# The end of attention in a two-layer block: output products in parts, weight splits placed last, a norm's chunks spread

## The reference, cut to what matters

```python
for l in range(DEPTH):                      # DEPTH = 2
    xn = _rms_norm(x, attn_norm[l])
    h = xn @ w_in[l]
    ...
    o_a = _dense_causal_attention(...)      # "mla", 4 heads of 64
    o_b = _dense_causal_attention(...)      # "fox"
    o_c = _moba_attention(...)              # "moba"
    o_d = _diff_causal_attention(...)       # "diff"
    o_d = _rms_norm(o_d, diff_sub_norm[l]) * (1.0 - lam_init)
    o_e = _memory_attention(...)            # "mem"
    mixed = jnp.concatenate([_merge(o_a), _merge(o_b), _merge(o_c), _merge(o_d), _merge(o_e)], axis=-1)
    x = x + mixed @ w_o[l]
    xn = _rms_norm(x, ffn_norm[l])
    gate = _causal_dwconv(xn @ ffn_w_gate[l], ffn_conv_w[l], ffn_conv_b[l])
    x = x + (jax.nn.silu(gate) * (xn @ ffn_w_up[l])) @ ffn_w_down[l]
return x
```

## Time and profile before

| | us |
|---|---|
| median of 3 runs | 2453.97 (2451.75 to 2454.61) |
| the profiled execution's own time | 2455.71 |
| its span | 2453.7 |
| PE busy | 2374.2 (97%) |
| DVE busy | 1803.3 (73%) |
| ACT busy | 1371.4 (56%) |
| POOL busy | 130.9 (5%) |

### The profile page before, as it was taken

How to read it: one execution, slowest core, us unless ns; L and a number is a source line. 1 busy time by engine, 2 the same in 40 slices (tenths; PEclk the granted TensorE clock), 3 DMA queues, 4 the chain that set the end, 5 groups by cost and what they waited for, 6 DMA issues and landing times.

```text
span 2453.7 us, 33655 instructions
## 1 busy us (share of the span) xinstructions
PE 2374.2 (97%) x14448; PEld 2117.4 (86%) x14448; DVE 1803.3 (73%) x1835; ACT 1371.4 (56%) x1347; POOL 130.9 (5%) x107
## 2 busy tenths in 40 slices
PE   5999999999999999999999999998998999998999
PEld 5999999788988888888888888876888999788999
DVE  5666566776688888888888888886575676665766
ACT  4345444464577777677777777765444344544433
POOL 2001000001100000000000000004110001201000
PEclk9999999999999999999999999999898999998999
DMA  5653546453499999999999999994233655332653
GB/s 191 190 188 122 188 149 223 129 195 123 157 365 354 355 345 348 351 358 347 353 348 357 347 356 350 355 342 138 82 108 103 206 173 178 112 104 72 194 182 104
DMA packets 309644, 566.92 MB, mean 231 GB/s; under 512 B 12338, under 2 KB 137553, under 8 KB 309360
## 3 DMA queue, kind: packets, MB, share of 16 engines
q1 hardware_dynamic: 305792, 560.39, 65.9%
q10 hardware_dynamic: 3696, 4.30, 0.5%
HBM read 563.60 MB, written 1.05 MB: 230 GB/s over the span
## 4 chain that ended last, share of the span: by engine, by line
PE 85%; DVE 7%; ACT 3%; DMA 3%; POOL 1%; issue 1%; ACTq 0%; DVEq 0%; SPq 0%; POOLq 0%
PE bank L996 22%; PE bank L787 15%; PE bank L1014 11%; PE bank L771 7%; PE bank L637 7%; PE bank L625 6%; PE bank L250 4%; PE bank L1317 3%; DVE wL L202 3%; PE bank L647 2%; PE bank L1266 2%; PE bank L613 2%; DMA raw<-in_od_moe_gu 2%; ACT wH L231 2%; DVE arena L202 1%
## 5 line engine op out<-in xcount | busy, mean ns | idle before, releaser
L202 DVE TENSOR_TENSOR wL<-raw,wH 128x2048 fp32r<-128x2048 f32 (+3 forms) x541 | 1211.3, 2246 | 379.9 <-ACT wH L231 377.2
L231 ACT ACTIVATE wH<-raw 128x2048 fp32r<-128x2048 f32 (+3 forms) x541 | 1014.4, 1877 | 562.8 <-PE bank L787 102.7
L996 PE MATMUL bank<-wH,ra 128*128 128x512 f32 x1792 | 577.6, 393 | 1.4 <-DVE wL L202 1.0
L996 PEld LDWEIGHTS bank<-wH,ra 128*128 128x128 f32 x1792 | 336.5, 188 | 73.2 <-DVE wL L202 2.2
L787 PE MATMUL bank<-ra,wH 128*128 128x256 f32 x2112 | 382.5, 283 | 0.0
L996 PE MATMUL bank<-wL,ra 128*128 128x512 f32 x896 | 348.8, 389 | 0.0
L787 PEld LDWEIGHTS bank<-ra,wH 128*128 128x128 f32 x2112 | 329.7, 192 | 1.1 <-issue 0.8
L787 PE MATMUL bank<-ra,wL 128*128 128x256 f32 x1056 | 298.8, 283 | 0.0
L1014 PE MATMUL bank<-wH,ra 128*128 128x512 f32 x896 | 286.6, 391 | 3.2 <-DVE ra L202 3.2
L637 PE MATMUL bank<-wH,ra 128*128 128x512 f32 (+2 forms) x800 | 228.4, 368 | 4.8 <-DVE ra L205 4.8
L787 PEld LDWEIGHTS bank<-ra,wL 128*128 128x128 f32 x1056 | 202.7, 192 | 0.0
(11 more groups left out here) (204 smaller groups left out, 2637.3 us busy)
## 6 DMA issues: line engine op xcount, KB each, us to landing
raw<-in_od_moe_gu SPq DMA_DIRECT2D x224, 1024.0 KB, 6.6
raw<-in_od_moe_down SPq DMA_DIRECT2D x112, 1024.0 KB, 6.7
raw<-in_ev_ffn_gu SPq DMA_DIRECT2D x22, 1024.0 KB, 5.2
raw<-in_ffn_w_gate SPq DMA_DIRECT2D x22, 1024.0 KB, 5.4
raw<-in_ffn_w_up SPq DMA_DIRECT2D x22, 1024.0 KB, 5.3
raw<-in_ffn_w_down SPq DMA_DIRECT2D x22, 1024.0 KB, 5.0
raw<-in_xa_wkv SPq DMA_DIRECT2D x16, 1024.0 KB, 5.2
raw<-in_od_pw_w SPq DMA_DIRECT2D x12, 1024.0 KB, 5.1
```

What stands on the lines that cost most here:

```text
L202: self.op.tensor_tensor(out, a, b, op).then_inc(*self.sig.up(name))
L231: self.op.activation(out, a, ACT.Copy, **kw).then_inc(*self.sig.up(name))
L996: m = p.op.matmul(out[:, :], a, b, start=half == 0 and c == 0 and i == 0, stop=half == 1 and c == 3 and i == 2)
```

## The change

Four edits, all in the order of work at the end of the attention of each layer. What is computed stays the same.

1. `pe_out_product` takes a range of its 16 steps. The products of fox and diff are cut in two halves, that of moba in 8, 4 and 4 steps, and the parts stand between turns, scores and values of quads 8 to 11. Diff's turn (`pe_out_turn`) moves from behind score 10 into the middle of fox's product. Score 11 moves behind turn 10.
2. The splits of the feed-forward's first gate and up blocks (`blocks("w_o", l, "moba")` and `"mem"`) move on ACT and DVE behind the high and low half of mem, the last of the attention.
3. The final norm's eight operations on DVE become four pairs, behind the maxima of quads 8, 9, 10 and 11.
4. The squares of diff's norm move ahead of `turned(8)`; ACT's and DVE's copies of diff's turn move up as the turn does (ahead of the mem split on ACT, ahead of `value(8)` on DVE).

```diff
@@ pe_second
         product = lambda *k: self.pe_out_product(p, s, l, *k)
...
-        self.pe_out_product(p, s, l, "mla")
+        product("mla")
         value(7)
         turn(8)
         score(9)
         self.pe_qk_turn(p, s, l, "mem")
-        self.pe_out_product(p, s, l, "fox")
+        product("fox", 0, 8)
+        self.pe_out_turn(p, s, "diff", 7)
+        product("fox", 8, 16)
         value(8)
         turn(9)
         score(10)
-        self.pe_out_turn(p, s, "diff", 7)
+        product("diff", 0, 8)
         value(9)
+        turn(10)
         score(11)
-        turn(10)
-        self.pe_out_product(p, s, l, "diff")
+        product("diff", 8, 16)
         self.pe_out_turn(p, s, "moba", 9)
         value(10)
         turn(11)
-        self.pe_out_product(p, s, l, "moba")
+        product("moba", 0, 8)
         value(11)
+        product("moba", 8, 12)
         self.pe_out_turn(p, s, "mem", 11)
-        self.pe_out_product(p, s, l, "mem")
+        product("moba", 12, 16)
+        product("mem")
@@ pe_out_product
-    def pe_out_product(self, p, s, l, g):
+    def pe_out_product(self, p, s, l, g, a=0, b=16):
...
-        for c, nb in [(c, nb) for nb in range(8) for c in range(2)] if last else [(c, nb) for c in range(2) for nb in range(8)]:
+        order = [(c, nb) for nb in range(8) for c in range(2)] if last else [(c, nb) for c in range(2) for nb in range(8)]
+        for c, nb in order[a:b]:
...
-        if not last:
+        if not last and b == 16:
             m.then_inc(*self.pe.up(("block", self.index["w_o", l, g])))
@@ act_second
         exp(9)
         self.act_turned(a, s, l, "mem")
+        self.act_out_turned(a, s, "diff")
         blocks("w_o", l, "diff")
         turned(9)
         exp(10)
-        self.act_out_turned(a, s, "diff")
         turned(10)
         exp(11)
-        blocks("w_o", l, "moba")
         self.act_out_turned(a, s, "moba")
         turned(11)
+        self.act_out_turned(a, s, "mem")
+        blocks("w_o", l, "moba")
         blocks("w_o", l, "mem")
-        self.act_out_turned(a, s, "mem")
@@ dve_second
+        def final_norm(c0):
+            if l == 0:
+                v.wait_ge(*self.act.of(("s0", "inv")))
+                for c in (c0, c0 + 1):
+                    v.stt(("s0", "h", c), self.hT[:, c, :], self.hT[:, c, :], self.col("final_norm", c), self.inv[:, :],
+                          ALU.mult, ALU.mult)
...
         top(8)
+        final_norm(0)
         blocks("w_o", l, "mla")
         self.dve_mean_heads(v, s, "mem_q", sqh[:, 0:512], 64)
         value(7)
+        self.dve_sub_squares(v, s)
         turned(8)
         top(9)
-        self.dve_sub_squares(v, s)
         self.dve_turned(v, s, l, "mem")
+        final_norm(2)
         blocks("w_o", l, "fox")
         self.dve_sub_norm(v, s, l)
...
+        self.dve_out_turned(v, s, "diff")
         value(8)
         turned(9)
         top(10)
+        final_norm(4)
         blocks("w_o", l, "diff")
-        self.dve_out_turned(v, s, "diff")
         value(9)
+        turned(10)
         top(11)
-        turned(10)
-        if l == 0:
-            v.wait_ge(*self.act.of(("s0", "inv")))
-            for c in range(C):
-                v.stt(("s0", "h", c), ...)
-        blocks("w_o", l, "moba")
+        final_norm(6)
         self.dve_out_turned(v, s, "moba")
         value(10)
         turned(11)
-        blocks("w_o", l, "mem")
         value(11)
         self.dve_out_turned(v, s, "mem")
+        blocks("w_o", l, "moba")
+        blocks("w_o", l, "mem")
```

More of the change, by code:

```diff
@@ L1116, in pe_second @@
         score, turn, value = (lambda n, f=f: f(p, s, n, quads[n]) for f in (self.pe_scores, self.pe_exp_turn, self.pe_values))
+        product = lambda *k: self.pe_out_product(p, s, l, *k)
         p.span = (4, 8)
@@ L1304, in pe_out_turn @@
                      [self.mixed[g][:, t, x * 128:(x + 1) * 128] for x, t in four], 128, self.dve, (s, "fm_lo", g))
-    def pe_out_product(self, p, s, l, g):
+    def pe_out_product(self, p, s, l, g, a=0, b=16):
         wh, wl = self.pe_block(p, ("w_o", l, g), 2)
-        at, n = 2 * GROUPS.index(g), 0
+        at, n = 2 * GROUPS.index(g), a
         first, last = g == GROUPS[0], g == GROUPS[-1]
         p.wait_ge(*self.dve.of((s, "fm_lo", g)))
-        for c, nb in [(c, nb) for nb in range(8) for c in range(2)] if last else [(c, nb) for c in range(2) for nb in range(8)]:
+        order = [(c, nb) for nb in range(8) for c in range(2)] if last else [(c, nb) for c in range(2) for nb in range(8)]
+        for c, nb in order[a:b]:
             if first and c == 0 and nb % 2 == 0:
@@ L1315, in pe_out_product @@
             ns = slice(nb * 128, (nb + 1) * 128)
-            for i, (a, b) in enumerate(passes(wh[:, c, ns], wl[:, c, ns], self.X10[0][:, at + c, :], self.X10[1][:, at + c, :])):
-                m = p.op.matmul(self.banks[nb // 2][:, (nb % 2) * 256:(nb % 2) * 256 + 256], a, b,
+            for i, (one, other) in enumerate(passes(wh[:, c, ns], wl[:, c, ns], self.X10[0][:, at + c, :], self.X10[1][:, at + c, :])):
+                m = p.op.matmul(self.banks[nb // 2][:, (nb % 2) * 256:(nb % 2) * 256 + 256], one, other,
                                 start=first and c == 0 and nb % 2 == 0 and i == 0, stop=last and c == 1 and i == 2,
@@ L2977, in dve_second @@
         top(10)
+        final_norm(4)
         blocks("w_o", l, "diff")
-        self.dve_out_turned(v, s, "diff")
         value(9)
+        turned(10)
         top(11)
-        turned(10)
-        if l == 0:
-            v.wait_ge(*self.act.of(("s0", "inv")))
-            for c in range(C):
-                v.stt(("s0", "h", c), self.hT[:, c, :], self.hT[:, c, :], self.col("final_norm", c), self.inv[:, :],
-                      ALU.mult, ALU.mult)
-        blocks("w_o", l, "moba")
+        final_norm(6)
         self.dve_out_turned(v, s, "moba")
```

## The result

The changed kernel takes 2437.82 us in the median of 5 runs (2435.98 to 2440.32); the kernel before, beside it, 2453.97 (5 runs, 2447.68 to 2454.71). The ratio is 0.994, 95% interval 0.9927 to 0.9954: 16.15 us faster, where 11.3 were forecast. The profiled execution took 2437.17 us, its span is 2435.4, the mean granted clock 0.986 (0.978 before).

A forecast was written before the change was run, and what follows sets the result against it. TensorE (PE) alone was taken as the bound, 85% of the span. Idle time 0.5 and 1.2 us plus clock 9.55 us gave 11.3 us: 2453.97 - 11.3 = 2442.7 us, range 2435 to 2452.5.

The forecast's parts named there:

- the signs: What the new trace should show in the two stretches: mean clock 0.95 or more, some 6 us idle each.
- Splits last: PE's waits ahead of moba's product, mem's turn and mem's product (1.93, 2.99, 1.41 us) all go: 6.33 us, both layers.
- The new wait at diff's turn: PE, after 8 of fox's 16 steps, waits for DVE's `sub`: 2.9 us in layer 0, 2.1 in layer 1.
- The norm in pairs: Final norm's DVE operations spread in pairs; the one cost is 0.81 us ahead of the moba split in layer 0.
- The tail: From mem's turn to L591: residual adds at T + 7.0, L591 at T + 16.7, PE idle some 3.5 us.
- Clock: Low-clock losses in both stretches shrink to one 1.7 us loss per layer, giving back 4.85 and 4.7 us.
- A: Clock does not recover in the stretches; only 1.7 us of idle time won: 2452.3 us, chance 0.14.
- B: Clock recovers wholly in both stretches, all 12.95 us of loss go: 2439.3 us, chance 0.17.
- C: Slower: low clock behind the `sub` wait and the tail's idle time, 10 us lost a layer: 2459.3 us, chance 0.06.
- D: Another wait takes over at mem, each 1.4 us plus 1.7 us of clock, 3 us a layer: 2448.7 us, chance 0.13.
- POOL's hold: Before L591, two `ra<-hT` on DVE held 1.1 us by POOL's add; by the skill's rule up to 1.30 us.

The follow-up runs named there:

- The splits alone: Kernel before with only the two feed-forward weight splits moved behind mem's halves, products whole and PE's order as before: 2437.98 us, ratio 0.9933.
- the kernel without the adds: Changed kernel with POOL's adds of squares for the feed-forward's norm replaced by one add on two columns, so the sum is incomplete: 2433.7 us, ratio 0.9927.
- the kernel with the parts alone: Changed kernel with both splits back at their old places and moba's last four steps ahead of mem's turn again: 2451.84 us, ratio 1.0002.
- one split back: Changed kernel with the gate block's split ahead of moba's halves again on ACT and DVE, the up block's split staying last: 2440.29 us, ratio 0.9933.

## Why the prediction held, point by point

The forecast was 2442.7 us in 2435.0 to 2452.5. Direction and mechanism were right, the size was short: the gain was 16.15 us for 11.3. The mean clock of 0.97 and 1.00 is as the signs had it (0.95 or more); the idle time is 5.3 and 4.5 us for some 6.

1. *Splits last: the three waits go.* Right, all 6.33 us in both layers. But that is the work of two edits. The splits alone remove 1.93 + 2.40 us and two of three low-clock pieces. The last 0.59 us and the 1.41 us are still there with the splits alone and gone in the whole change, where four steps of moba stand between value 11 and mem's turn and four behind the turn.
2. *The new wait at diff's turn.* 2.59 and 1.80 us for 2.9 and 2.1. I had the moba split start at 1816.74 + 5.38 = 1822.12 on the old clock, that is 7.99 us behind value 7; it starts 7.75 us behind (1819.06 - 1811.31), 0.24 us earlier. From there to diff's turn it takes 3.66 us for 3.52, so `sub` gains 0.1 us in all. The other 0.2 us is on PE, which is ready for the turn 8.82 us behind value 7 (1822.72 - 2.59 - 1811.31) where I had 8.63.
3. *The norm in pairs costs 0.81 us at one place.* Right: layer 0 waits 0.79 us longer than layer 1 at diff's turn, and alone it changes nothing.
4. *The tail.* From the end of mem's turn, T = 1849.94, the residual adds come at T + 7.0 as forecast and L591 at T + 16.9 for 16.7. The idle time is 2.67 us for 3.5: I gave PE's sixteen feed-forward steps 5.8 us, and they take 6.8, since a first step behind each wait is longer (0.50 for 0.40 us, and the next matmul starts later). Without those waits, in the kernel without the adds, they take 1865.47 - 1859.64 = 5.83 us. That L591 came out so well is luck. I took 9.7 us from the first residual add to L591 as work of DVE, ACT and POOL. But in the kernel before, PE ran its sixteen steps there without a wait (1870.35 to 1876.41), and L591 came 2.0 us behind the last `ra<-hT` (1876.41 - 1874.39) because PE was still at them; now it comes 0.9 us behind (1866.80 - 1865.92). Against these 1.1 us too many, and a wait of 0.15 us for PE that the earlier trace rows did not show, stand 1.5 us too few: DVE is held by POOL for 2.9 us where it was 1.4, as told below.
5. *Clock: a term that was mis-sized.* "I keep one such loss per layer": layer 0 keeps it, 1.7 us to the digit, behind the new wait; layer 1 keeps none. The first low stretch, behind score 11 and turn 10, is gone too.

The largest misses are those of points 4 and 5. The sum in the terms of the forecast: idle time gave back 1.7 + 2.4 = 4.0 us where 1.7 was forecast (2.3 more, from points 2 and 4), and busy time 5.1 + 6.1 = 11.2 where 9.55 was (1.7 more, the loss that layer 1 didn't keep). Together 15.3; the remaining 0.9 us of the median is within what runs differ by outside the stretches. Of the 2.8 us by which value 7 comes earlier in the profiled execution, nothing is credited: the second profile of the kernel before had it earlier still, at 1807.43.

**The rivals.** A (no clock recovery) is excluded by the earlier trace rows against the one piece left. B, the whole recovery, had 2439.3 us, nearer to the measured 2437.82 than the forecast's 2442.7: layer 1 does it, layer 0 does not. B's number kept the forecast's 1.7 us of idle time, though, where 4.0 were won, so it too is near in part by luck. C needed over 14 us at the low level in a layer; there are 3.9. Its mechanism exists, though: without the splits' move, the new stalls and the old ones add up and eat all the clock gained. D did not happen: mem's product waits for nothing.

**POOL's hold.** I took one hold of 1.1 us from the earlier trace rows; that row shows one add of four. The others of the kernel before, DVE first, then POOL:

```profile
1872.34 2.05 DVE L205 SCALAR_TENSOR_TENSOR ra<-hT,cols,ra 128x256 fp32r<-128x256 f32 x4
...
1871.47 1.44 POOL L202 TENSOR_TENSOR sq<-sq 128x512 f32<-128x512 f32 x1 [0.40 <-ACT sq L228]
1874.02 2.34 POOL L202 TENSOR_TENSOR sq<-sq 128x512 f32<-128x512 f32 x2 [1.11 <-ACT sq L228]
```

Four `ra<-hT` took 2.05 us there, 0.3 more than the 1.77 of four with POOL quiet; one add ended soon after they began, and the next began as they ended. With the 1.1 us that makes 1.4 us of hold. In the new order four `ra<-hT` stand beside all four adds, and the test without adds gives 2.9 us on DVE and 2.0 us per layer on PE. So the hold goes by how the two engines' work falls together, and the forecast's sum did not let it grow. The Trainium skill, page "SBUF — State Buffer", section "Who interferes with whom", has DVE instructions with two SBUF inputs and GpSimd's reads exclude each other for a whole instruction. The trace agrees in size: four `ra<-hT` last 4.68 us beside four adds of 1.26 us each, where four without adds take 1.77.

## What to carry to other kernels

Where engines work through hand-written lists, look for work of the next stage that stands ahead of the present stage's last small steps, above all where it waits for a buffer that those very steps free: moving it behind gave over two thirds of the gain here, by the stretches, with no other edit. Price each removed wait twice, as idle time and as the low-clock piece that may stand behind it: 1.7 us here behind waits of 1.9 to 2.6 us. And a transpose moved up to overlap a product must not be moved past the arrival of its input: half a product later it was free, and where the change put it, it cost 4.2 us in layer 0 and 1.9 in layer 1. Last, before the time of a stretch is moved to a new place in a sum, see which engine set its end: here 9.7 us that were put down to DVE and POOL ended with PE's own steps.

## What the runs showed of the hardware

The drop to the lower of TensorE's two levels does not follow the length of the wait alone. At the 2.59 to 2.60 us ahead of diff's turn the granted clock fell in all six profiles that have this wait in layer 0 (0.56 over 3.9 us in the changed kernel); at the 1.79 or 1.80 us at the same place in layer 1 it stayed at 1.00 in all six. It fell behind 1.93 us at moba's product before, but not behind the 2.49 us there in layer 0 of the kernel with the parts alone, and it fell behind 2.49 us in its layer 1 and behind 2.50 us in both layers with one split back. Behind the 1.59 us ahead of L787 it fell in none of the five profiles that have it.

The changed kernel, layer 1, behind the 1.80 us:

```profile
2204.60:2208.50 3.90, 3.90 (x34) 3.90 (x35) 0.69 (x1) 0.95 (x2) 0.00 (x0) 1.00 0.79 257
```

The kernel with the parts alone, behind its two waits of 2.49 us:

```profile
1843.20:1847.20 4.00, 3.99 (x34) 3.99 (x34) 0.97 (x3) 0.00 (x0) 0.00 (x0) 1.00 0.75 262
2230.90:2234.10 3.20, 3.20 (x18) 3.20 (x17) 0.00 (x0) 0.00 (x0) 0.00 (x0) 0.50 0.77 301
```

And it fell behind 0.48 us in score 11, where turn 10 and value products stand around the wait, in each profile that keeps this order. What decides it between these is left open; it was not tried by itself.
